# Three norm stages of a two-layer kernel cut into chunks of 512 columns, with the next weight panels split inside them

## What is computed

```
u = conformer_conv(rms_norm(h, g_mix_pre))          # ends in u @ w_out + b_out
h = h + rms_norm(u, g_mix_post)                     # first norm stage: two norms in a row
u = swiglu(rms_norm(h, g_ffn_pre))                  # w_gate, w_up, w_down, 5632 hidden
h = h + rms_norm(u, g_ffn_post)                     # second norm stage: two norms in a row
x = h[meta:]
proj = rms_norm(x, g_norm1) @ w_in                  # q, k, forget gate, pool input, v, gates
...                                                 # attention, pooling, gated merge
x = x + merged @ w_out_2
x = x + peer(rms_norm(x, g_norm2))                  # third norm stage, then query projection, expert gathers
```

## Time and profile before

| | |
|---|---|
| median of 3 executions | 3153.6 us (3149.84 to 3153.75) |
| the profiled execution's own time | 3150.34 us |
| its span, first to last instruction | 3148.6 us |
| TensorE busy | 2678.1 us (85%) |
| VectorE busy | 1867.8 us (59%) |
| ScalarE busy | 1281.5 us (41%) |
| GpSimd busy | 790.6 us (25%) |
| mean granted TensorE clock | 0.919 of full speed |

### The profile page before, as it was taken

One profiled execution on the slowest core, in us unless ns is written; L12 is line 12 of the kernel. 1 busy time (PEld: TensorE's weight loads), 2 busy tenths in 40 slices (PEclk: granted clock), 3 DMA queues, 4 the chain that ended last, 5 costly groups with the idle time before them and its releaser, 6 DMA issues.

```text
span 3148.6 us, 43578 instructions
## 1 busy us (share of the span) xinstructions
PE 2678.1 (85%) x16136; PEld 2120.7 (67%) x16136; DVE 1867.8 (59%) x2652; ACT 1281.5 (41%) x2465; POOL 790.6 (25%) x559
## 2 busy tenths in 40 slices
PE   8999799999999979989999899878846657777773
PEld 6886689999999969979998797555523422222220
DVE  5888455555555554674444468888756654545455
ACT  2003444444444444335333354555457752322223
POOL 0000000000000000030000003554756677556556
PEclk9999899999999989999999999999966678888887
DMA  6342435555555534334555547999999899999999
GB/s 234 134 147 108 160 139 185 185 186 187 187 187 187 187 133 165 130 121 147 187 180 195 185 171 276 369 393 384 395 372 350 329 359 411 410 408 404 407 399 354
DMA packets 128247, 790.56 MB, mean 251 GB/s; under 512 B 30963, under 2 KB 30963, under 8 KB 32131
## 3 DMA queue, kind: packets, MB, share of 16 engines
q0 software_dynamic: 74944, 408.84, 33.0%
q1 hardware_dynamic: 53168, 380.06, 32.8%
HBM read 921.18 MB, written 4.19 MB: 294 GB/s over the span
## 4 chain that ended last, share of the span: by engine, by line
PE 50%; DVE 15%; DMA 14%; issue 9%; POOL 6%; ACT 4%; DVEq 1%; POOLq 0%; SPq 0%; ACTq 0%
PE bank L1594 14%; PE bank L1595 14%; PE bank L1596 14%; DMA s_u<-in_expert_u,s_u_index 8%; DMA s_v<-in_expert_v,s_v_index 6%; DVE s_product_out L1483 4%; PE bank L1675 4%; POOL s_u L534 3%; POOL s_v L549 3%; PE bank L1961 3%; DVE s_cacc L1083 1%; DVE s_w_lo L1001 1%; DVE s_yrow L1203 1%; ACT s_one_key L951 1%; ACT s_w_hi L571 1%
## 5 line engine op out<-in xcount | busy, mean ns | idle before, releaser
L1001 DVE TENSOR_TENSOR s_w_lo<-s_raw,s_w_hi 128x2048 fp32r<-128x2048 f32 x258 | 591.8, 2294 | 625.6 <-ACT s_w_hi L571 625.1
L571 ACT ACTIVATE s_w_hi<-s_raw 128x2048 fp32r<-128x2048 f32 x256 | 490.2, 1915 | 642.1 <-PE bank L1596 642.0
L1594 PE MATMUL bank<-s_a_hi,s_w_hi 128*128 128x256 f32 x2560 | 722.8, 282 | 10.7 <-DVE s_w_lo L1001 6.5
L1595 PE MATMUL bank<-s_a_lo,s_w_hi 128*128 128x256 f32 x2560 | 722.6, 282 | 0.0
L1596 PE MATMUL bank<-s_a_hi,s_w_lo 128*128 128x256 f32 x2560 | 721.8, 282 | 0.0
L1961 PE MATMUL bank<-s_v,s_spread 128*32 128x512 f32 x2048 | 322.7, 787 | 332.3 <-DMA s_v<-in_expert_v,s_v_index 306.5
L1594 PEld LDWEIGHTS bank<-s_a_hi,s_w_hi 128*128 128x128 f32 x2560 | 486.0, 190 | 15.3 <-DVE s_w_lo L1001 9.2
L1596 PEld LDWEIGHTS bank<-s_a_hi,s_w_lo 128*128 128x128 f32 x2560 | 486.8, 190 | 0.0
L1595 PEld LDWEIGHTS bank<-s_a_lo,s_w_hi 128*128 128x128 f32 x2560 | 482.9, 189 | 1.4 <-issue 1.0
L1483 DVE CUSTOM_DVE_ANT_0 s_product_out<-s_u,s_xn_late 128x2048 f32<-128x2048 f32 x128 | 293.9, 2296 | 278.2 <-DMA s_u<-in_expert_u,s_u_index 277.9
L1961 PEld LDWEIGHTS bank<-s_v,s_spread 128*32 128x32 f32 x2048 | 83.5, 139 | 547.5 <-issue 516.9
(11 more groups left out here) (305 smaller groups left out, 3124.1 us busy)
## 6 DMA issues: line engine op xcount, KB each, us to landing
s_raw<-in_stream SPq DMA_DIRECT2D x292, 1024.0 KB, 4.8
s_raw<-in_dense_u SPq DMA_DIRECT2D x32, 1024.0 KB, 8.9
s_raw<-in_expert_v SPq DMA_DIRECT2D x32, 1024.0 KB, 8.8
s_u<-in_expert_u,s_u_index POOLq DMA_INDIRECT x256, 13.7
s_v<-in_expert_v,s_v_index POOLq DMA_INDIRECT x256, 14.5
s_xres<-in_x SPq DMA_DIRECT2D x2, 1024.0 KB, 6.5
out<-s_out_row SPq DMA_DIRECT2D x8, 256.0 KB, 4.8
s_bout_row<-in_b_out POOLq DMA_DIRECT2D x1, 1024.0 KB, 8.7
```

The source lines that it names most:

```text
L571: act.activation(w_hi[s % 2][:, :], raw[s][:, :], ACT.Copy).then_inc(hi_ready, 1)
L1001: dve.tensor_tensor(w_lo[s % 2][:, :], raw[s][:, :], w_hi[s % 2][:, :].bitcast(f32), ALU.subtract)\
L1594: pe.matmul(dst, left[0], right[0], start=start, stop=False)
L1595: pe.matmul(dst, left[0], right[1], start=False, stop=False)
```

## The change

- **Squares by chunk.** `sums_of_squares` becomes `chunk_squared`: 512 columns at a time, each with its own sum in the new tile `parts`; DVE adds the four sums of a row (`mean_sum`), and ACT's root takes scale 1/D and the eps as bias (`mean_root`). In `w_out` and `w_out_2` ACT squares the columns of round i-1 behind its first split of round i, the last columns at the end; in the last round of `ffn` bank by bank.
- **Root table early.** `early_root` does one throwaway Sqrt before the last squares.
- **Gains early.** In `w_out` DVE multiplies `gained` by chunk, each round (`post(None, ...)`). The second `post(gffn_row, ...)` does two chunks before and six chunks behind the reciprocal.
- **Two engines scale.** In `post` ACT scales t = 0 and DVE t = 1 (`xs_late_ready`), by chunks. In `post_2` DVE makes `xn` from `xres` in one instruction per chunk, and `xs` goes.
- **By groups of features.** Transposes and both copies out go b by b, with t inside. TensorE does groups 0 and 1, the first bank of the projection's panel 0, then groups 2 and 3 (`between`), then the rest of panel 0.
- **Splits inside.** `split_hi(0)` goes behind the first root; `split_lo(0)` between groups 1 and 2 (before group 3 in `post_2`). In the last round of `ffn` DVE leaves out its last split and does it in `post` (`split_lo(-1)`), so that the 8 bank adds come at once.
- **Loops.** The first `ffn` round stands apart and copies to `yrow` where the others add, so the memsets go; ACT and DVE also have the last one apart; `qk`'s first round stands apart; `w_out_2` is written out on ACT and DVE. `gained` and the squares move to other places.

```diff
-            def sums_of_squares(src, junk, ready=None):
...
+            def chunk_squared(src, junk, t, c, first):
+                part = slice(c * 512, (c + 1) * 512)
+                return act.activation(junk[:, t, part], src[:, t, part], ACT.Square, accum_out=parts[:, first + 4 * t + c:first + 4 * t + c + 1])
...
+            def mean_root(k):
+                act.wait_ge(ms_ready, n.after("ms", k))
+                act.activation(stat[:, 4:4 + TT], stat[:, 0:TT], ACT.Sqrt, scale=1.0 / D, bias=stat[:, 8:9]).then_inc(root_ready, 1)
+            def early_root():
+                act.activation(stat[:, 10:11], stat[:, 10:11], ACT.Sqrt)
...
+            def rows_squared(i):
+                for t in range(TT):
+                    act.wait_ge(bank_empty[t], n.after(f"empty{t}", 0))
+                    ins = chunk_squared(yrow, squares, t, i, 0)
+                return ins
...
+                        if i and c == 0:
+                            rows_squared(i - 1)
+            early_root()
+            rows_squared(3).then_inc(ssq_ready, 1)
...
+            def post(gain):
+                mean_root(1)
+                split_hi(0)
+                for c in range(4):
+                    for t in range(TT):
+                        act.wait_ge(res_ready, n.after("res", 2 * c + t + 1))
+                        ins = chunk_squared(xres, squares, t, c, 8)
+                ins.then_inc(ssq_ready, 1)
+                mean_root(2)
                 act.wait_ge(rstd_ready, n.after("rstd", 1))
-                for t in range(TT):
-                    act.activation(xs[:, t, :], xres[:, t, :], ACT.Copy, scale=stat[:, 4 + t:5 + t])\
-                        .then_inc(xs_ready, 1)
-                transposed_hi(gain, 0)
+                for c in range(4):
+                    part = slice(c * 512, (c + 1) * 512)
+                    act.activation(xs[:, 0, part], xres[:, 0, part], ACT.Copy, scale=stat[:, 4:5]).then_inc(xs_ready, 1)
+                transposed_hi(gain)
...
             def post(row, gain):
...
+                if row:
+                    gains(0, 0)
+                    gains(0, 1)
+                mean_sum(1, 0)
                 dve.wait_ge(root_ready, n.after("root", 1))
                 link(dve.reciprocal(stat[:, 4:4 + TT], stat[:, 4:4 + TT]))
+                if row:
+                    for t, c in ((1, 0), (1, 1), (0, 2), (1, 2), (0, 3), (1, 3)):
+                        gains(t, c)
+                    settled()
+                for c in range(4):
+                    part = slice(c * 512, (c + 1) * 512)
+                    for t in range(TT):
+                        dve.scalar_tensor_tensor(xres[:, t, part], gained[:, t, part], stat[:, 4 + t:5 + t], xres[:, t, part],
+                                                 ALU.mult, ALU.add).then_inc(res_ready, 1)
+                mean_sum(2, 8)
                 inverse(2)
+                dve.wait_ge(rstd_ready, n.after("rstd", 1))
+                for c in range(4):
+                    part = slice(c * 512, (c + 1) * 512)
+                    dve.tensor_scalar(xs[:, 1, part], xres[:, 1, part], stat[:, 5:6], None, ALU.mult).then_inc(xs_late_ready, 1)
+                if row:
+                    split_lo(-1)
+                for b in range(4):
+                    if b == 2:
+                        split_lo(0)
+                    transposed_lo(gain, b)
-            for t in range(TT):
-                link(dve.memset(yrow[:, t, :], 0.0))
...
             with n.rounds(dve, "post_2"):
+                mean_sum(1, 8)
+                inverse(1)
...
                 for c in range(4):
+                    part = slice(c * 512, (c + 1) * 512)
+                    for t in range(TT):
+                        dve.scalar_tensor_tensor(xn[:, t, part], xres[:, t, part], stat[:, 4 + t:5 + t], g2_row[:, part],
+                                                 ALU.mult, ALU.mult).then_inc(xn_ready, 1)
+                    if c:
+                        transposed_lo(None, c - 1)
+                split_lo(0)
+                transposed_lo(None, 3)
...
-                for c in range(8, 12):
+                for c in range(8, 11 if last else 12):
                     split_lo(c)
...
+                    if first:
+                        dve.tensor_copy(dst, bank[b][:, :]).then_inc(bank_empty[b], 1)
+                    else:
+                        dve.tensor_tensor(dst, dst, bank[b][:, :], ALU.add).then_inc(bank_empty[b], 1)
...
+            with n.rounds(dve, "ffn"):
+                ffn(True)
+            with n.rounds(dve, "ffn", FF // 512 - 2):
+                ffn(False)
+            with n.rounds(dve, "ffn"):
+                ffn(False, True)
...
+            def halves(late=False):
+                at = marks()
+                transposes(0, at, late)
+                transposes(1, at, late)
+                def rest():
+                    transposes(2, at, late)
+                    transposes(3, at, late)
+                return rest
...
+                        if between and c == 0 and j == 0:
+                            between()
```

More of the change, by code:

```diff
@@ L717, in _ @@
                     split_hi(c)
+            with n.rounds(act, "ffn"):
+                ffn(True)
+            with n.rounds(act, "ffn", FF // 512 - 2):
+                ffn(False)
+            with n.rounds(act, "ffn"):
+                ffn(False)
+                early_root()
+                for b in range(8):
+                    act.wait_ge(bank_empty[b], n.after(f"empty{b}", 2))
+                    ins = chunk_squared(yrow, squares_ffn, b < 4, b % 4, 0)
+                ins.then_inc(ssq_ready, 1)
             with n.rounds(act, "post"):
-                post(7, "g_norm1")
+                post("g_norm1")
             def copies_out(i, dst, offset):
@@ L1173, in _, with ffn @@
             with n.rounds(dve, "post"):
-                post(gmix_row, "g_ffn")
-            for t in range(TT):
-                link(dve.memset(yrow[:, t, :], 0.0))
-            with n.rounds(dve, "ffn", FF // 512):
+                post(None, "g_ffn")
+            def ffn(first, last=False):
                 for blk in range(2):
@@ L1182, in _ @@
                     for c in range(4):
-                        split_lo(c0 + c)
+                        if blk or c or not first:
+                            split_lo(c0 + c)
                     for j in range(2):
@@ L1209, in _ @@
             dve.tensor_tensor(wf_lo[:, :, :], wf_raw[:, :, :], wf_hi[:, :, :].bitcast(f32), ALU.subtract).then_inc(wflo_ready, 1)
[L1210 removed]
+            with n.rounds(dve, "qk"):
+                for c in range(1, 4):
+                    split_lo(c)
+            with n.rounds(dve, "qk", 3):
                 for c in range(4):
@@ L1747, in _ @@
             with n.rounds(pe, "post"):
-                transposes(xs, xs_ready, "xs")
+                rest = halves()
             ready = [n.after(f"empty{b}", 0) for b in range(4, 8)]
-            with n.rounds(pe, "qk", 4):
-                feature_major((0, 1, 2, 3), tokens, 0, 4, 4, 0, ready=ready)
+            with n.rounds(pe, "ffn"):
+                ffn(rest, ready)
+            with n.rounds(pe, "ffn", FF // 512 - 1):
+                ffn(None, None)
+            with n.rounds(pe, "post"):
+                rest = halves()
+            ready = [n.after(f"empty{b}", 0) for b in range(4, 8)]
+            with n.rounds(pe, "qk"):
+                feature_major((0, 1, 2, 3), tokens, 0, 4, 4, 0, ready=ready, between=rest)
+            with n.rounds(pe, "qk", 3):
+                feature_major((0, 1, 2, 3), tokens, 0, 4, 4, 0)
             with n.rounds(pe, "forget"):
@@ L1876, in _ @@
             with n.rounds(pe, "post_2"):
-                transposes(xn, xn_ready, "xn")
+                rest = halves(late=True)
             ready = [n.after(f"empty{b}", 0) for b in range(4, 8)]
```

202 lines of the change are left out of this document (106 added, 96 removed).

## The result

The changed kernel takes 3113.41 us (median of 4, 3111.01 to 3114.02) against 3152.69 before (median of 4): ratio 0.9875, 95% interval 0.9858 to 0.9892. It is faster by 39.3 us, where 26 were forecast; the range ended at 3120. The profiled execution took 3111.01, its span is 3109.2.

A forecast was written before the change was run, and what follows sets the result against it. TensorE, busy 85% of the span, was taken as the bound, idle in one hole per norm stage while the norm chain ran; gains of 13.4 + 6.0 + 6.6 = 26.0 us gave 3126, range 3120 to 3140.

The forecast's parts named there:

- First stage: Norm stage behind `w_out`: shorter norm chain lets panel 0 start at 390.9 and panel 1 end at 405.9; gain 13.4 us.
- 1.9 of idle time: First stage: TensorE idle 1.9 us between groups 0 and 1's transposes and panel 0, followed by slow matmuls.
- Second stage: Norm stage behind `ffn`: panel 0 done at 1182.4, where the next panel started at 1188.44; gain 6.0 us.
- Third: Norm stage behind `w_out_2`: DVE carries everything, panel 0 ends at 1818.5, where panel 1 started at 1825.15; gain 6.6 us.
- the wait of 1.0 for group 3's `xn`: Third stage: TensorE waits for group 3's `xn` with banks 1 to 3 queued behind, costing 1.0 us.
- The prices: Costs per instruction: 512 columns take 0.60 us on ACT, 0.61 on DVE with two tensors, 0.66 with a scalar.
- The clock: First stage's panel 0: TensorE at the low clock for 3.1 us, 15 matmuls, then fast.
- Rival 1: Clock stays low through all of panel 0 and its transposes: 14 of the 26 us lost, 3140; chance 0.13.
- The table load: Root's table load of 1.28 us leaves the first stage's path; none remains between last square and root.
- the sum: Gains of the three norm stages added, 13.4 + 6.0 + 6.6 = 26.0 us, giving 3126.
- At no cost: Column squares and gains moved inside `w_out` and `w_out_2` lie in idle time; uncovered they would cost 8.4 us.
- Rival 2: Gain given back in the last 1200 us of gathers and transfers, ending at 3151; chance 0.05.

The follow-up runs named there:

- run 12: Changed kernel with GpSimd multiplying three of the second stage's `gained` chunks and DVE doing three ahead of the root: 3114.3 us, ratio 0.9888 to the kernel before.
- run 13: Changed kernel with a 64-byte gap that lands 448 of 512 gathers off 256 bytes, dense loads on it, measured again: 3122.8 us, ratio 0.9912 to before.
- run 9: Changed kernel with all 32 transposes of a norm stage ahead of panel 0: 3115.9 us, ratio 0.9890 to the kernel before.
- run 10: Changed kernel without the three `early_root` calls: 3115.6 us, ratio 0.9891 to the kernel before.
- run 1: Kernel before plus an unused 64-byte tile where the change puts `parts`: 3141.1 us, ratio 0.9972 to the kernel before.
- run 2: Changed kernel with `parts` laid over a dead tile, so other tiles keep their old addresses: 3121.1 us, ratio 0.9907 to the kernel before.
- run 5: Changed kernel with 64 unused bytes more ahead of `xres`, off a multiple of 256: 3121.0 us, ratio 0.9896 to the kernel before.
- run 6: Changed kernel with 128 unused bytes more ahead of `xres`, off a multiple of 256: 3123.6 us, ratio 0.9906 to the kernel before.
- run 7: Changed kernel with 256 unused bytes more ahead of `xres`, on a multiple of 256: 3115.0 us, ratio 0.9875 to the kernel before.
- run 11: Changed kernel with a 64-byte gap that lands 448 of 512 gathers off 256 bytes, dense loads on it: 3122.9 us, ratio 0.9917 to the kernel before.
- run 14: Changed kernel with a 64-byte gap placing dense loads off 256 bytes and 448 of 512 gathers on it: 3118.4 us, ratio 0.9900 to the kernel before.
- run 15: The changed kernel measured again, unaltered: 3114.6 us, ratio 0.9888 to the kernel before.

## Why the prediction was right and wrong

- **The stages together**: 26.1 where 26.0 was forecast.
- **First stage, 13.4**: measured 13.24. Transposes at 383.85 (forecast 385.7 less 1.6 of an earlier start), first product at 388.99 (390.9 less 1.6), panel 0 done 25.06 behind `w_out`'s end, as forecast. Groups 2 and 3 were just in time, as forecast. Small errors cancel: 18 slow matmuls and not 15 cost 0.3, the second half's transposes took 1.67 and not 1.9. That it fits to 0.2 is luck in part: in runs 12 and 13, with the same stage, the clock was up before panel 0 and the stage took 29.9, a gain of 14.5. That 16 transposes behind half a panel leave a hole ahead of it, which they could fill, was in the forecast as 1.9 of idle time and not seen as a price (run 9).
- **Second stage, 6.0**: 5.68 at panel 0, 6.25 at panel 1. **Third, 6.6**: 7.17. In the third DVE has no idle time from the reciprocal on until group 3 is out, as forecast; the wait of 1.0 for group 3's `xn` that was given to TensorE did not come. The prices held: a 512-column square starts 0.61 after the last (0.60 taken), the residual's 8 chunks took 5.39 (5.3), and six gain chunks 3.70. The estimate by the Trainium skill, "VectorE: DVE Perf Modes", section "The TRN2 errata", 0.69 for each, would have made those six 4.1.
- **The clock**: 1.2 GHz for 18 matmuls where 15 were given, then 2.4. Rival 1 did not come. Nor does the rule of the Trainium skill, "TensorE: Matmul & The Clock Gate", section "Part 4: PE-mode transpose", that would have made it: in run 9, where TensorE does nothing but transposes from 385.52 to 391.39, the granted clock is 0.50 until 390, 0.76 from 390 to 391 and 1.00 from there. Runs 12 and 13 against after show that the moment of its rise moves the first stage by 1.3 us between kernels.
- **The table load**: there is none between last square and root, but its worth was overrated; run 10 puts it at 0.5 in all (-0.22, -0.41, +1.09).
- **Ahead of the stages** 1.6 us more came, and between them 0.4, nothing of which was in the sum: `w_out` ends at 373.29 instead of 374.89. Its end lies at 373.1 to 379.3 in the kernels here, so this belongs to no step of the change.
- **The step that failed** is "At no cost", and with it the sum. It went through what is moved on queues and engines, and ended at the third stage. That the new tile `parts` moves the addresses of all tiles behind it, the landing places of 1200 us of DMA-bound transfers among them, is in no term. Rival 2 asked of that phase only if it could take a gain back, not if it could give one. The phase gave 11.3 in the profiles, of which 7 are the addresses (runs 1, 2, 5 to 7) and the rest the scatter of this phase. By which of the moved tiles they act is open. With the old addresses the change gives 3121.1 (run 2), in the range and 4.9 under the forecast; by its ratio of 0.9907 it would be 3123.4 beside the 3152.7 of the first comparison.

## What to carry to other kernels

Where a phase is bound by DMA, look at the byte address at which its targets start, before and after an edit: a tile of 64 bytes ahead of them moved this kernel by 8 us, as much as a norm stage rewritten, and a large buffer placed on a multiple of 256 costs nothing. Compare a change with a version at the same addresses before putting its gain down to its logic. A queue in the order in which data is made is not always the shortest: 16 transposes put behind half a panel left TensorE idle for 1.5 us ahead of it, which they could have filled, and where their data comes last of all the same split was right.

## What the hardware showed that was not expected

- With the tiles from `xres` on, the landing places of 8 KB rows among them, off a multiple of 256 bytes: 0.6% more time for a phase with DMA at a mean share of 0.97, the same at 64, 128 and 192, and as much in the packets of the gathers' queue (1039.7 us on the mean against 1032.3).
- A GpSimd tensor_tensor on two SBUF tiles (2048 columns, 4.79 us) held up a DVE instruction with two SBUF inputs for 4.25 us. DVE's adds out of PSUM ran beside GpSimd's products with no loss (8 in 5.45 us with them and without).
- The gap of runs 11, 13 and 14 made `ffn` 4.3 us longer, with TensorE never idle (run 13: 469 or 470 matmuls in most windows of 66.6 us, run 15: 473). Why the products stream slower is open.
